# Two-part fp32r projections of a two-block transformer: aligned operands, 512-column moving weights, and gate rows kept in another order

## What is computed

```python
# block one
p_l = modulate(x, norm1_g, mod[:, 0], mod[:, 1]) @ w_in      # 1024 -> 7040, context tokens too
pool_l, q_l, k_l, v_l, rw_l, gate_l = split_cols(p_l, IN_SPLITS)
merged = sum(sigmoid(gate_l[n]) * (branch[n] @ w_br[n]))      # pool, attention, rwkv
x = x + mod[:, 2] * (merged @ w_out)                          # gate row (0, 2)
x = x + mod[:, 5] * hier_moe(modulate(x, norm2_g, ...))       # gate row (0, 5), 32 experts
# block two, layers 0 and 1, for latent tokens and (layer 0) context tokens
x = x + g1 * mixer(norm(x) * (1 + sc1) + sh1)                 # w_in_0 ... w_out_0; MLA ... mla_w_o
x = x + g2 * conv_ffn(norm(x) * (1 + sc2) + sh2)              # ffn_up 1024 -> 5632, ffn_down 2816 -> 1024
return rmsnorm(x, final_norm)
```

## Time and profile before

| | |
|---|---|
| median of 3 runs | 4074.56 us (4073.24 to 4076.42) |
| the profiled execution: its own time | 4076.78 us |
| its span, first to last instruction | 4074.7 us |
| mean granted TensorE clock | 0.927 |
| PE busy | 3555.5 us (87%) |
| PE weight loads busy | 2833.6 us (70%) |
| VectorE, ScalarE, GpSimd busy | 41%, 22%, 1% |
| DMA | 487 MB, 120 GB/s on average |

### The profile page before, as it was taken

One profiled execution on the slowest core, in us unless ns is written; L12 is line 12 of the kernel. 1 busy time (PEld: TensorE's weight loads), 2 busy tenths in 40 slices (PEclk: granted clock), 3 DMA queues, 4 the chain that ended last, 5 costly groups with the idle time before them and its releaser, 6 DMA issues. The chain is left out here.

```text
span 4074.7 us, 70734 instructions
## 1 busy us (share of the span) xinstructions
PE 3555.5 (87%) x31158; PEld 2833.6 (70%) x31158; DVE 1669.7 (41%) x2880; ACT 914.4 (22%) x1524; POOL 37.5 (1%) x40
## 2 busy tenths in 40 slices
PE   5969997776988899996989877899999978989998
PEld 3858995655846666554755846888879965577888
DVE  3654544372214211113444337444443354245543
ACT  2035531031301111112111133211122212323322
POOL 0000000000000000000000000000000000000000
PEclk8979997888999799998999988999999989999999
DMA  6130004402344599994531201143432110013322
GB/s 228 57 130 4 4 4 158 135 1 75 104 146 149 232 409 413 410 411 168 181 107 47 52 13 32 53 124 114 124 96 68 42 49 26 1 42 93 94 91 91
DMA packets 275844, 487.13 MB, mean 120 GB/s; under 512 B 12394, under 2 KB 191115, under 8 KB 266868
## 3 DMA queue, kind: packets, MB, share of 16 engines
q1 hardware_dynamic: 268468, 457.91, 32.5%
q0 software_dynamic: 1984, 16.81, 1.1%
q10 hardware_dynamic: 5120, 8.39, 0.6%
HBM read 453.68 MB, written 29.39 MB: 119 GB/s over the span
## 5 line engine op out<-in xcount | busy, mean ns | idle before, releaser
L373 PE MATMUL banks<-leading,w_rest 128*128 128x512 f32 (+2 forms) x1920 | 699.9, 365 | 65.6 <-DVE w_rest L312 65.6
L373 PE MATMUL banks<-rest,w_leading 128*128 128x512 f32 (+2 forms) x1920 | 691.1, 360 | 0.0
L373 PE MATMUL banks<-leading,w_leading 128*128 128x512 f32 (+2 forms) x1920 | 690.8, 360 | 0.0
L312 DVE TENSOR_TENSOR w_rest<-land,w_leading 128x1024 fp32r<-128x1024 f32 (+2 forms) x328 | 307.1, 978 | 449.5 <-ACT w_leading L299 449.5
L373 PEld LDWEIGHTS banks<-leading,w_rest 128*128 128x128 f32 (+1 forms) x1920 | 364.6, 190 | 136.3 <-DVE w_rest L312 52.5
L299 ACT CAST w_leading<-land 128x1024 fp32r<-128x1024 f32 (+2 forms) x328 | 263.2, 850 | 869.7 <-DMA land<-in_w_in 323.1
L373 PE MATMUL banks<-w_rest,leading 128*128 128x256 f32 (+3 forms) x1332 | 396.6, 298 | 53.1 <-DVE w_rest L312 53.1
L373 PEld LDWEIGHTS banks<-leading,w_leading 128*128 128x128 f32 (+1 forms) x1920 | 364.7, 190 | 59.0
L373 PEld LDWEIGHTS banks<-rest,w_leading 128*128 128x128 f32 (+1 forms) x1920 | 364.7, 190 | 57.6
L373 PE MATMUL banks<-w_leading,rest 128*128 128x256 f32 (+3 forms) x1332 | 391.8, 294 | 0.0
L373 PE MATMUL banks<-w_leading,leading 128*128 128x256 f32 (+3 forms) x1332 | 391.1, 294 | 0.0
(11 more groups left out here) (555 smaller groups left out, 5166.9 us busy)
## 6 DMA issues: line engine op xcount, KB each, us to landing
wg<-in_w_exp_gate SPq DMA_DIRECT2D x32, 2048.0 KB, 12.6
wu<-in_w_exp_up SPq DMA_DIRECT2D x32, 2048.0 KB, 14.7
wd<-in_w_exp_down SPq DMA_DIRECT2D x32, 2048.0 KB, 11.8
ws<-in_ada_w SPq DMA_DIRECT2D x96, 512.0 KB, 3.8
land<-in_w_in SPq DMA_DIRECT2D x41, 1024.0 KB, 5.6
land<-in_ffn_up SPq DMA_DIRECT2D x44, 512.0 KB, 5.3
land<-in_ffn_up SPq DMA_DIRECT2D x88, 256.0 KB, 3.3
land<-in_ffn_down SPq DMA_DIRECT2D x24, 768.0 KB, 4.3
```

Source lines behind the costliest of these rows:

```text
L312: nc.vector.tensor_tensor(rest[s % 2][:, k0:k1, 0:n], slots[s % wslots][:, k0:k1, 0:n], leading[s % 2][:, k0:k1, 0:n].bitcast(F32), ALU.su ...
L373: mm = nc.tensor.matmul(bank_of(r, kind, at), lhsT, rhs, start=(k == 0 and q == 0), stop=(k == kt - 1 and q == len(each) - 1))
```

## The change

1. `two_parts` and the two parts of the weights are allocated on multiples of 512 bytes. The exceptions are `ffn_down_0`'s (the `whole` case), both on 32 bytes. In the built program 5556 fp32r matmuls of 512 columns, 2232 of 256 and all 240 of 320 or 384 then have both operands on multiples of 64; the 792 of `ffn_down_0`, now of 512 columns, have both 32 bytes past one.
2. Two jobs of kind N of 256 columns are joined into one of 512 columns, with half the contraction per step. The 4944 matmuls concerned (768 in attention, 192 pool, 384 `w_out`, 576 `w_out_0`, 1584 `ffn_down_0`, 384 `mla_w_o`, 1056 `ffn_down_1`) become 2472.
3. `keep_gate_rows` copies each vector together on GpSimd and writes 8 (for one row twice 4) neighbouring floats per partition: 128 pieces of 32 bytes in place of 1024 of 4. The row in DRAM is then in the order p*8+f, and the consumers read it with a stride of 8 (4 for the experts) elements.
4. Steps are cut evenly (`bounds`); `ffn_down_0` has 2 jobs of 8 steps in place of 4 of 4, `ffn_down_1` 2 of 6 in place of 4 of 4. Side work is spread over visits of steps in place of results. The squares of `ffn_down_1` follow each result, so that only one tile is left for `closing`.

```diff
-    return [ctx.enter_context(nc.sbuf_tensor(f"{name}_{nc.next_id()}", [P, k, tokens], F32R, side=side)) for name in ("leading", "rest")]
+    return [ctx.enter_context(nc.sbuf_tensor(f"{name}_{nc.next_id()}", [P, k, tokens], F32R, side=side, align_bytes=512)) for name in ("leading", "rest")]
...
+    return [(w_in[:, 2048:2048 + 256], 0, KD, 256), (w_in[:, 512:1024], 0, KD // 2, 512), (w_in[:, 0:512], 0, KD // 2, 512),
+            (w_in[:, 3968:3968 + 256], 0, KD, 256), (a["w_out"][:, 0:512], 0, KD // 2, 512),
...
+    bounds = [-(-kt * q // k_chunks) for q in range(k_chunks + 1)]
+    steps = [(j, w, n, results, k0, k1) for j, (w, n, results) in enumerate(jobs) for k0, k1 in zip(bounds, bounds[1:])]
...
-        leading, rest = [[ctx.enter_context(nc.sbuf_tensor(f"{name}_{nc.next_id()}", [P, size, width], F32R)) for _ in range(2 if split else 0)]
+        leading, rest = [[ctx.enter_context(nc.sbuf_tensor(f"{name}_{nc.next_id()}", [P, size, width], F32R, align_bytes=32 if whole is not None else 512)) for _ in range(2 if split else 0)]
...
+                        for t in sides_between(ends[s] + i, ends[s] + i + 1):
+                            side_piece(pe, t)
...
-def keep_gate_rows(m, pool, i):
-
-
-    for row, (block, chunk, kind) in enumerate(GATE_ROWS):
-        if block == i:
-            pool.dma_start(m.gate_dram[row].rearrange("(f p) -> p f", p=P), m.mod[:, i, KD * chunk:KD * (chunk + 1), kind], allow_slow_non_contiguous=True).then_inc(m.gate_kept_sem, 16)
-            m.gates_kept += 16
+def keep_gate_rows(nc, m, pool, i):
+
+
+    rows = [row for row, of in enumerate(GATE_ROWS) if of[0] == i]
+    for q, row in enumerate(rows):
+        chunk, kind = GATE_ROWS[row][1:]
+        nc.gpsimd.tensor_copy(m.gate_columns[:, q, :], m.mod[:, i, KD * chunk:KD * (chunk + 1), kind]).then_inc(m.gate_column_sem, 1)
+        m.gate_columns_made += 1
+    pool.wait_ge(m.gate_column_sem, m.gate_columns_made)
+    for q, row in enumerate(rows):
+        n = m.gate_run[row]
+        pool.dma_start(m.gate_dram[row].rearrange("(h p f) -> p h f", p=P, f=n), m.gate_columns[:, q, :].rearrange("p (h f) -> p h f", f=n)).then_inc(m.gate_kept_sem, 16)
+        m.gates_kept += 16
...
+            jobs = [(a["w_in"][:, 512 + c:512 + c + 512], 512, [("N", t, 512) for t in range(NTC if c < 512 else 0, NT)])
+                    for c in range(0, 3 * 512, 512)]
...
+            products(nc, m, jobs, hT_of(m), evac, "vector", banks=6, split=True, width=512, k_chunks=2, side=modulation_tiles(m, a, 0, 16, 48))
...
+        products(nc, m, [(a["w_in"][:, 0:512], 512, [("N", NTC + t, 512) for t in range(NTL)])], hT_of(m), evac, "scalar",
+                 split=True, width=512, k_chunks=2)
...
-            chain(nc.vector.tensor_tensor(b.t[:, turn[0], 0:width], out, b.gate[:, kind, c], ALU.mult))
+            gate = b.gate[:, kind, :].rearrange("q (p f) -> q f p", f=KD)[:, width // P * j:width // P * (j + 1), :]
+            chain(nc.vector.tensor_tensor(b.t[:, turn[0], 0:width].rearrange("q (f p) -> q f p", p=P), out.rearrange("q (f p) -> q f p", p=P), gate, ALU.mult))
             return nc.vector.tensor_tensor(x[:, c], x[:, c], b.t[:, turn[0], 0:width], ALU.add)
...
-            if r >= len(tiles):
-                before, (t, x, kind) = j - 1, tiles[r % len(tiles)]
-                act.wait_ge(read_sem, r - len(tiles) + 1)
-                if r >= len(tiles) + 2:
-                    act.wait_ge(aux_sem, r - len(tiles) - 1)
-                nc.scalar.activation(squares[0][:, r % 2, 0:width], x[:, width * before:width * (before + 1)], ACT.Square,
-                                     accum_out=squares[1][:, r % len(tiles), before:before + 1]).then_inc(aux_sem, 1)
+            if r:
+                of, (t, x, kind) = (r - 1) // len(tiles), tiles[(r - 1) % len(tiles)]
+                act.wait_ge(read_sem, r)
+                if r >= 2:
+                    act.wait_ge(aux_sem, r - 1)
+                nc.scalar.activation(squares[0][:, 0:width], x[:, width * of:width * (of + 1)], ACT.Square,
+                                     accum_out=squares[1][:, (r - 1) % len(tiles), of:of + 1]).then_inc(aux_sem, 1)
...
+                        nc.vector.tensor_tensor(y[u][:, :].rearrange("q (f p) -> q f p", p=P), m.ps[:, 5 + u, :].rearrange("q (f p) -> q f p", p=P),
+                                                e.gate[:, :].rearrange("q (p f) -> q f p", f=4), ALU.mult).then_inc(y_read_sem, 1)
...
-                    project_add(nc, m, a["w_out_0"], of_halves((hi, lo)), KD, adds, (1, 2, n), split=True, width=256, by_tile=(m.mixT, hi, lo, 0))
+                    project_add(nc, m, a["w_out_0"], of_halves((hi, lo)), KD, adds, (1, 2, n), split=True, banks=8, k_chunks=2, by_tile=(m.mixT, hi, lo, 0))
...
-                    project_add(nc, m, a["ffn_down_1"], of_halves(m.fT, first), KF, adds, (2, 5, n), width=256, split=True, banks=8, k_chunks=4,
+                    project_add(nc, m, a["ffn_down_1"], of_halves(m.fT, first), KF, adds, (2, 5, n), split=True, banks=8, k_chunks=6,
...
-                    project_add(nc, m, a["ffn_down_0"], of_halves((leading, rest)), KF, adds, (1, 5, n), width=256, split=True, banks=8, k_chunks=4, whole=(m.fT, leading, rest),
-                                pooled=lambda pool: keep_gate_rows(m, pool, 2))
+                    project_add(nc, m, a["ffn_down_0"], of_halves((leading, rest)), KF, adds, (1, 5, n), split=True, banks=8, k_chunks=8, whole=(m.fT, leading, rest),
+                                pooled=lambda pool: keep_gate_rows(nc, m, pool, 2))
...
-                for t in range(NTL):
-                    if t >= 2:
-                        act.wait_ge(squared_sem, t - 1)
-                    nc.scalar.activation(m.final_junk[:, t % 2, 0:256], m.x[:, t, last], ACT.Square, accum_out=m.final_ss[:, t, 3:4]).then_inc(squared_sem, 1)
+                t = NTL - 1
+                nc.scalar.activation(m.final_junk[:, :], m.x[:, t, last], ACT.Square, accum_out=m.final_ss[:, t, 1:2]).then_inc(squared_sem, 1)
...
+        m.gate_run = [4 if row == (0, 5, 0) else KD for row in GATE_ROWS]
```

More of the change, by code:

```diff
@@ L182, in products @@
         wslots = LAND // (size * width)
-    steps = [(j, w, n, results, k0, min(k0 + size, kt)) for j, (w, n, results) in enumerate(jobs) for k0 in range(0, kt, size)]
+    bounds = [-(-kt * q // k_chunks) for q in range(k_chunks + 1)]
+    steps = [(j, w, n, results, k0, k1) for j, (w, n, results) in enumerate(jobs) for k0, k1 in zip(bounds, bounds[1:])]
     ends = [0]
@@ L186, in products @@
         ends.append(ends[-1] + len(step[3]))
-    total = sum(len(results) for w, n, results in jobs)
     with ExitStack() as ctx:
@@ L218, in sides_between @@
                 n = PIECES * len(side)
[L219 removed]
+                return range(-(-r0 * n // ends[-1]), -(-r1 * n // ends[-1]))
             @block.sync
@@ L397, in each_result @@
                             between(eng, s + 1)
+                        if of_visit is not None:
+                            of_visit(eng, ends[s] + i)
                         if k1 == kt:
@@ L406, in read, with sides_read @@
                 evac(bank_of(r, kind, at), j, at, chain).then_inc(read_sem, 1)
-            def read_both(dve, r, count, j, kind, at):
-                for t in sides_between(r, r + 1):
+            def sides_read(dve, visit):
+                for t in sides_between(visit, visit + 1):
                     u = t // PIECES
@@ L415, in read_both, with read_here @@
                         side_add(dve, u - 1)
+            def read_here(dve, r, count, j, kind, at):
                 if evac_on == "vector":
@@ L1002, in block_one @@
             hi, lo = two_parts(nc, mix, KD, LAT)
-            project_add(nc, m, a["w_out"], of_halves((hi, lo)), KD, [(t, m.x[:, t, :], 0) for t in range(NTL)], (0, 2, 1), split=True, width=256,
+            project_add(nc, m, a["w_out"], of_halves((hi, lo)), KD, [(t, m.x[:, t, :], 0) for t in range(NTL)], (0, 2, 1), split=True, banks=8, k_chunks=2,
                         by_tile=(m.merged, hi, lo, 0), early=next_rows, late=rows_landed(m))
@@ L1051, in evac @@
         def evac(out, j, at, chain):
-            return nc.scalar.copy(m.u[:, at[0] - NTC, 256 * j:256 * (j + 1)], out)
-        products(nc, m, [(a["w_in"][:, c:c + 256], 256, [("N", NTC + t, 256) for t in range(NTL)]) for c in (0, 256)], hT_of(m), evac, "scalar",
-                 split=True, width=256)
+            return nc.scalar.copy(m.u[:, at[0] - NTC, :], out)
+        products(nc, m, [(a["w_in"][:, 0:512], 512, [("N", NTC + t, 512) for t in range(NTL)])], hT_of(m), evac, "scalar",
+                 split=True, width=512, k_chunks=2)
         with stage(nc, weights=1, banded=2, diffed=1, copied=1, mapped=1, read=1) as (
@@ L1831, in merge @@
         products(nc, m, jobs, hT_of(m), lambda out, j, at, chain: nc.scalar.activation(
```

(9 more changed lines are left out.)

41 lines of the change are left out of this document (15 added, 26 removed).

## The result

| | before | after |
|---|---|---|
| median of the runs | 4073.9 us (4068.9 to 4076.4) | **4016.2 us** (4014.4 to 4017.2) |
| ratio to before | 1 | 0.9859, 95% interval 0.9842 to 0.9876 |
| span of the profiled execution | 4074.7 us | 4012.6 us |

The change takes 57.7 us off, 1.4%. Measured a second time, with its own runs of before beside it, it takes 4016.9 against 4068.4 us: ratio 0.9871 (0.9855 to 0.9888), 51.4 us. The forecast was 3948 us, a gain of 126.6 us: more than double of what came. The sign was right. The range (3925 to 4022) held only because it had been drawn wide enough to take in rival 1, *only the relative position counts*, which had said 4011 us; the likeliest case alone had ended at 3968 us.

The account below looks back on a forecast made before the run. PE's stream of matmuls was taken to bound the projections. Matmul prices 111.5 us plus gate rows 15.9 less small terms 0.8 gave 126.6 us off, 3948 us on the scale of the medians; range 3925 to 4022 us.

Parts of the forecast that it names:

- rival 1: fp32r matmuls: only the operands' relative position counts, aligned ones cost 226.6 and 120.0 ns; 4011 us, chance 0.35.
- the likeliest case alone: Whole kernel: the forecast of 3948 us with its own range, 3925 to 3968 us; chance 0.47, a third rival included.
- the price of an aligned fp32r matmul: Projections: with both operands aligned, 218.5 ns at 512 columns and 111.9 at 256, from 5.2 ns of fixed cost.
- Joining: Passes of 256 columns joined into 512: 13.4 ns saved per pair with operands as they lay, 10.6 us in `ffn_down_0`.
- Gate rows: Gates and mLSTM input stages: PE's stalls for weights behind the 4-byte writes, and the half clock after, go: 15.9 us.
- rival 3: Gate writes still hold up the weights: 15.9 us of the gain stay away, 3964 us; chance within the forecast's 0.47.
- The strided read: VectorE's multiply by the gate row: 3% more by a PSUM row; were it a doubling, 3.5 us at five tails.
- Small terms: Start of `ffn_down_0` some 2 us less, `ffn_down_1` +0.5, wider last results +3.2, `closing` -0.9: net 0.8 us lost.
- The slower rival: Aligned matmuls: the weight load no longer fits beside the stream, 325 ns at 512 columns; 4787 us, chance 0.04.

Follow-up runs that it names:

- the two versions at 512 columns: The changed kernel, and the same with each gate row laid out once in column order by a GpSimd copy: 4016.9 and 4010.4 us, measured side by side.

## Why the prediction was right, and where it failed

- **The failed step is the price of an aligned fp32r matmul: "I take this 5.2 ns, as the one aligned row".** It put 218.5 and 111.9 ns; 226.6 and 120.0 were measured. The 5.2 ns were what was left in a stream of 128 columns after a weight load that I read as 106.7 ns; there the load sets the pace and not the columns, and it says nothing of a stream in which the columns do. Read again, the trace held the better guide: 13.3 ns at 256 and at 512 columns, in both stages where the operands matched. The runs showed that fp32r carries this constant wherever both operands start equally, on a multiple of 64 or not. The mistake was to look for the cause in the alignment of each operand, when the rows in hand differed in whether the two were *equal*. With 226.6 and 120.0 ns in the sum its matmul part is 48.0 in place of 111.5 us, as rival 1 has it. That is 63.5 of the 69 us between the forecast gain of 126.6 and the 57.7 measured. The experiment with the alignment alone agrees: 13.6 us, where the forecast's price would have given 93. (The sum also counted 48 matmuls as aligned whose operands still started 32 bytes apart, a term of under 1 us.)
- **Rival 1** had the mechanism and its numbers (226.6, 120.0 ns) and came within some 5 us. It was given 0.35, the forecast 0.47. Its argument against itself, that the price "vanishes" when the stationary operand alone is aligned, misread 118.2 and 233.2: mismatched streams are slower by 6.6 ns at 512 columns and quicker by 1.8 at 256; they don't lose a fixed cost.
- **Joining**: 13.4 ns per pair was right to 0.1 ns, the sum 25.8 in place of some 31 us (33.1 less 3% and the small terms). I had not looked at the q, k, v projection by itself, where fp32 pieces lie between the results and most of the stream behind them runs at 232 ns.
- **Gate rows**: the stalls were priced right, 15.9 against 17.8 us, and none came back, so rival 3, which would also have ended within the range, fell. The strided read was left out of the sum and priced at 3.5 us on a condition. The row it went by was a read of PSUM with a stride (3% more); the operand that now has the stride is in SBUF: 1.12 in place of 0.69 us, and 6.5 us in all by the medians of the two versions at 512 columns. The Trainium skill's rule (Advanced Engine Details and Errata, SBUF Cachelines) is that accesses each to another 16-byte line pay a penalty; the 1094 ns against 692 agree with it.
- **Small terms**: the start of `ffn_down_0` (2.0 us) and `closing` (1.0 us) came as worked out.
- **The slower rival** (the load no longer beside the stream) did not happen: PEld is busy 82.81 of 100 us beside a PE without idle time, as before.

## What to carry to other kernels

A fixed cost per instruction is read from streams that are bound by the same thing; a stream bound by its weight loads says nothing of one bound by its columns. When two rows differ in price, list everything in which they differ, the relation between the operands too, before naming one cause, and if one cheap part of the change can tell the causes apart, try it alone first. And a layout that saves a write's pieces moves them into a strided read: pay that once, on an idle engine, not at each use.

## What the runs showed of the hardware

- An fp32r matmul with its own load costs columns / 2.4 + 13.3 ns at full clock, if both operands start equally modulo 256 bytes: 226.6 ns at 512 columns, 120.0 at 256. bf16 costs 215.9 at 512, in the same place. (Of unequal addresses that agree modulo 256, the pair 0 and 256 was tried.)
- Unequal starts, 16 to 128 bytes apart, cost 231.7 to 234.1 ns at 512 columns. At 256 they cost less than equal ones: 118.2 ns in the kernel before, 113.6 where they were 64 bytes apart.
- Behind a piece of fp32 matmuls a stream with equal starts runs at 232 ns per 512 columns, in three cases of four until the next piece, 12 matmuls later; the cause is open.
- VectorE with one fp32 operand in SBUF at a stride of 32 or 16 bytes: 1.12 and 1.09 us for 512 elements, 0.69 without. GpSimd's strided copy of 1024 takes 2.75 us.
- Behind writes of 2048 pieces of 4 bytes a load of 1 MB reached ScalarE 14.9 us after its issue, over 9 us more than the median of such loads. Behind the same writes in 384 pieces of 32 and 16 bytes, which land in 2.0 to 2.3 us, it took 6.6 us and no matmul waited for it.
